# A hybrid encoder block in split float32: the two products with the high part of a weight tile put ahead of the one with the low part, and the memory rows loaded feature-wise

## The reference

```
h = rms_norm(x);  c_q, c_kv, k_rope, u_in, gate_a, gate_b = split(h @ w_in)
y_a = latent attention(c_q, c_kv, k_rope), 16 heads, chunk-causal
y_b = pointwise(silu(layer_norm(causal depthwise conv(glu(u_in)))))
x += (sigmoid(gate_a) * y_a + sigmoid(gate_b) * y_b) @ w_o
mem_n = rms_norm(mem)                      # 256 memory rows
k, v = split(mem_n @ w_kv_mem);  q = rms_norm(x) @ w_q_mem     # 4 heads of 512
x += softmax(q k^T * 512**-0.5) v @ w_o_mem
x += (silu(rms_norm(x) @ w_gate) * (rms_norm(x) @ w_up)) @ w_down   # d_ff 5632
return rms_norm(x)
```

## Time and profile before

| | us |
|---|---|
| median of 3 runs | 1680.53 (1680.05 to 1681.03) |
| the profiled execution | 1680.31 |
| its span, first to last instruction | 1678.5 |
| TensorE busy | 1662.8 (99% of the span) |
| VectorE, ScalarE, GpSimd busy | 1091.0, 818.9, 108.2 |
| TensorE weight loads | 1383.5 |
| TensorE's granted clock | 0.999 of full speed |

### The profile page before, as it was taken

How to read it: one execution, slowest core, us unless ns; L and a number is a source line. 1 busy time by engine, 2 the same in 40 slices (tenths; PEclk the granted TensorE clock), 3 DMA queues, 4 the chain that set the end, 5 groups by cost and what they waited for, 6 DMA issues and landing times.

```text
span 1678.5 us, 23555 instructions
## 1 busy us (share of the span) xinstructions
PE 1662.8 (99%) x7692; PEld 1383.5 (82%) x7692; DVE 1091.0 (65%) x1396; ACT 818.9 (49%) x1053; POOL 108.2 (6%) x160
## 2 busy tenths in 40 slices
PE   9999999999999999999999999999999999999998
PEld 8888888888888888878888788888888888888886
DVE  5555777678887457884448856666666666654453
ACT  7455655555545444555435644444444444344343
POOL 5100100011000000120001200000000000000000
PEclk9999999999999999999999999999999999999999
DMA  7865555555566655554445666666666666565563
GB/s 233 272 193 168 169 164 153 167 158 161 174 210 181 197 187 183 179 194 148 135 137 177 191 196 194 191 190 187 190 199 199 192 196 189 191 221 187 178 214 133
DMA packets 161284, 309.70 MB, mean 185 GB/s; under 512 B 10308, under 2 KB 17074, under 8 KB 160977
## 3 DMA queue, kind: packets, MB, share of 16 engines
q1 hardware_dynamic: 158864, 301.50, 57.8%
q0 software_dynamic: 1776, 6.47, 1.0%
q10 hardware_dynamic: 592, 1.06, 0.2%
HBM read 306.89 MB, written 2.10 MB: 184 GB/s over the span
## 4 chain that ended last, share of the span: by engine, by line
PE 92%; DVE 4%; issue 2%; ACT 1%; DMA 0%; DVEq 0%; SPq 0%; ACTq 0%; POOLq 0%; POOL 0%
PE acc L346 27%; PE acc L348 27%; PE acc L347 27%; DVE w_lo L1236 2%; PE tp L358 2%; DVE x_f L1549 1%; PE sc L675 1%; PE acc L569 1%; PE sc L491 1%; PE acc L571 1%; PE acc L570 1%; ACT w_hi L779 1%; PE acc L549 0%; PE acc L551 0%; PE acc L550 0%
## 5 line engine op out<-in xcount | busy, mean ns | idle before, releaser
L1236 DVE TENSOR_TENSOR w_lo<-raw,w_hi 128x1024 fp32r<-128x1024 f32 (+3 forms) x591 | 718.4, 1221 | 477.2 <-ACT w_hi L779 468.1
L779 ACT ACTIVATE w_hi<-raw 128x1024 fp32r<-128x1024 f32 (+3 forms) x591 | 606.5, 1029 | 767.3 <-PE acc L348 732.1
L346 PE MATMUL acc<-w_hi,crossT 128*128 128x512 f32 x832 | 325.7, 391 | 0.8 <-DVEq L1567 0.8
L348 PE MATMUL acc<-w_hi,crossT 128*128 128x512 f32 x832 | 323.9, 389 | 0.0
L347 PE MATMUL acc<-w_lo,crossT 128*128 128x512 f32 x832 | 323.8, 389 | 0.0
L346 PE MATMUL acc<-w_hi,mixT 128*128 128x512 f32 x796 | 315.5, 396 | 1.2 <-DVEq L1567 0.7
L348 PE MATMUL acc<-w_hi,mixT 128*128 128x512 f32 x796 | 310.5, 390 | 0.0
L347 PE MATMUL acc<-w_lo,mixT 128*128 128x512 f32 x796 | 310.1, 390 | 0.0
L346 PEld LDWEIGHTS acc<-w_hi,crossT 128*128 128x128 f32 x832 | 156.2, 188 | 33.7 <-issue 1.6
L348 PEld LDWEIGHTS acc<-w_hi,crossT 128*128 128x128 f32 x832 | 156.2, 188 | 32.7
L347 PEld LDWEIGHTS acc<-w_lo,crossT 128*128 128x128 f32 x832 | 156.2, 188 | 32.0
(11 more groups left out here) (244 smaller groups left out, 1350.9 us busy)
## 6 DMA issues: line engine op xcount, KB each, us to landing
raw<-in_w_in_dram SPq DMA_DIRECT2D x104, 512.0 KB, 3.7
raw<-in_w_gate_dram SPq DMA_DIRECT2D x88, 512.0 KB, 4.3
raw<-in_w_up_dram SPq DMA_DIRECT2D x88, 512.0 KB, 3.8
raw<-in_w_down_dram SPq DMA_DIRECT2D x80, 512.0 KB, 3.8
raw<-in_w_kv_mem_dram SPq DMA_DIRECT2D x64, 512.0 KB, 3.9
raw<-in_w_o_dram SPq DMA_DIRECT2D x32, 512.0 KB, 4.0
raw<-in_w_q_mem_dram SPq DMA_DIRECT2D x32, 512.0 KB, 3.7
raw<-in_w_o_mem_dram SPq DMA_DIRECT2D x32, 512.0 KB, 3.9
```

The source lines that it names most:

```text
L346: mm(o, lo, whi, start=first and k == 0, stop=False)
L348: ins = mm(o, hi, whi, start=False, stop=end)
L779: fn(w_hi[:, s, 0:width], raw[:, s, 0:width], ACT.Copy).then_inc(hi_done, 1)
L1236: V.tensor_tensor(w_lo[:, s, 0:width], raw[:, s, 0:width], w_hi[:, s, 0:width].bitcast(F32), ALU.subtract).then_inc(lo_done, 1)
```

## The change

- `products`: in each tile but a chunk's last it waits for `hi_done` alone, does the eight products with `w_hi` (for each bank and block low activations, then high ones), then waits for `lo_done` and does the four products with `w_lo`. The wait for `acc_free[1]` of a chunk's first tile stands in front of bank 1 as before. The last tile of a chunk is as it was. `tile_products` and `kv_products` (queries, keys and values of a pair) are as they were.
- The memory rows come from HBM already feature-wise (`memT`), as do the gains (`vecs`) and the taps (`w_dwT`); they are laid out outside the program. The 32 transposes of the memory rows and those of the gains and taps are gone. `operand_hi` and `operand_lo` make the parts on ScalarE and VectorE from `xs`. The squares of the memory rows are added up on VectorE (`fold_squares`, four additions) and summed over partitions by two products with a column of ones in the first pair.
- The memory attention: queries, keys, values and probabilities are split too, so each float32 product of 256 columns becomes three of the reduced type. This adds copies on ScalarE (`head_hi`, and the high part of the probabilities) and subtractions on VectorE (`head_lo` and others).
- Tables (`PAIR_*`, `HEAD_*`) say behind which tile a step of `attention` and of `mem_attention` stands in the loops. In H's first chunk the steps 0 to 4 stand behind tiles 0 to 4 as before.
- The bias row of the pointwise product is loaded at the start of D instead of in B.

```
+PAIR_PE = {1: (0, 1), 3: (2,), 6: (5,), 7: (7,)}
+PAIR_ACT = {1: (0, 1), 4: (3,), 6: (5,)}
+PAIR_DVE = {3: (2,), 4: (3,), 7: (7,)}
+HEAD_PE = {0: (0,), 2: (1,), 5: (3,), 6: (4,)}
+HEAD_ACT = {0: (0,), 2: (1,), 5: (3,), 6: (4,)}
+HEAD_DVE = {0: (0,), 2: (1,), 3: (2,), 5: (3,), 6: (4,)}
...
+                if not last:
+                    pe.wait_ge(hi_done, base + (t + 1))
+                    for b in range(NB):
+                        if first and not (isinstance(chunk, int) and chunk == 0):
+                            pe.wait_ge(acc_free[b], chunk)
+                        for k in range(kt):
+                            whi = w_hi[:, s, k * n:(k + 1) * n]
+                            for j in (1, 0):
+                                mm(acc[:, b, 0:n], lhs[j][:, k0 + k, b * P:(b + 1) * P], whi,
+                                   start=first and k == 0 and j == 1, stop=False)
+                    pe.wait_ge(lo_done, base + (t + 1))
+                    for b in range(NB):
+                        for k in range(kt):
+                            ins = mm(acc[:, b, 0:n], lhs[0][:, k0 + k, b * P:(b + 1) * P], w_lo[:, s, k * n:(k + 1) * n],
+                                     start=False, stop=False)
+                    ins.then_inc(tile_done, 1)
+                    return
                 pe.wait_ge(lo_done, base + (t + 1))
                 for b in range(NB):
-                    if first and not (isinstance(chunk, int) and chunk == 0):
-                        pe.wait_ge(acc_free[b], chunk)
                     for k in range(kt):
                         hi = lhs[0][:, k0 + k, b * P:(b + 1) * P]
                         lo = lhs[1][:, k0 + k, b * P:(b + 1) * P]
...
+                    if first and t == 5:
+                        pe.wait_ge(consts_made, 2)
+                        pe.wait_ge(sq_added, 1)
+                        for b in range(NB):
+                            ins = mm(xt[:, b:b + 1], sqT[:, 0, b * P:(b + 1) * P], ones[:, :], start=True, stop=True)
+                        ins.then_inc(sq_out, 1)
...
+                    for step in PAIR_PE.get(t, ()) if not first else ():
+                        attention(step, i - 1, i + (Q_C - 1))
...
-                    if last and t == 0:
-
-                        turn_x(0, Q_M0)
-                        turn_x(1, Q_M0)
                 kv_products(i * 12 + T_C, i * 3 + (C_C + 2))
-                if last:
-                    turn_x(2, Q_M0 + 1)
-                    turn_x(3, Q_M0 + 1)
 
             def kv_products(base, chunk):
...
+                    pe.wait_ge(key_lo, h + 1)
                     for b in range(NB):
                         for k in range(4):
-                            ins = mm(sc[:, 0, b * TOK:(b + 1) * TOK], memqT[:, k, b * P:(b + 1) * P],
-                                     memKT[:, cols(h * 4 + k, 1), :].rearrange("p o t -> p (o t)"),
-                                     start=k == 0, stop=k == 3)
+                            o = sc[:, 0, b * TOK:(b + 1) * TOK]
+                            hi, lo = (memqT[j][:, k, b * P:(b + 1) * P] for j in range(2))
+                            mm(o, lo, key_h[0][:, k, :], start=k == 0, stop=False)
+                            mm(o, hi, key_h[1][:, k, :], start=False, stop=False)
+                            ins = mm(o, hi, key_h[0][:, k, :], start=False, stop=k == 3)
...
+            def operand_hi(g):
+
+                dst, k0 = mem_rows(g)
+                for k in range(2):
+                    ins = fn(dst[0][:, k0 + k, :], mem_k[:, 2 * g + k, :], ACT.Copy, scale=vcol("norm_mem", 2 * g + k))
+                ins.then_inc(mem_hi, 1)
...
+                    if last and t == 9:
+                        act.wait_ge(tile_done, i * 12 + (T_C + 8))
+                    if last and t in (9, 11):
+                        operand_hi(t // 2 - 2)
+                    for step in PAIR_ACT.get(t, ()) if not first else ():
+                        attention(step, i - 1, i + (Q_C - 1))
...
+            def head_hi(t, h):
+
+                if t == 5:
+                    if not (isinstance(h, int) and h == 0):
+                        act.wait_ge(m_scores, h)
+                    fn(key_h[0][:, :, :], memKT[:, cols(h * 4, 4), :], ACT.Copy).then_inc(key_hi, 1)
+                if t == 6:
+                    if not (isinstance(h, int) and h == 0):
+                        act.wait_ge(m_pv, 2 * h)
+                    fn(val_h[0][:, :, :], memV[:, :, cols(h * CH, CH)], ACT.Copy).then_inc(val_hi, 1)
```

More of the change, by code:

```diff
@@ L235, in program @@
             ("m_norm", "m_turned", "m_out", "m_pv", "o_hi", "o_done"))
+        key_hi, key_lo, val_hi, val_lo, m_out_hi = (sem(n) for n in
+            ("key_hi", "key_lo", "val_hi", "val_lo", "m_out_hi"))
         x_new, x_turned, x_gained, x_hi_out, x_lo_out = (sem(n) for n in
@@ L705, in _ @@
                     turn_stage(Q_F, 2 * (S_F + 4))
-            for c in range(1, 4):
+            with pe.Fori(1, 4) as c:
                 for t in range(8):
                     products(c * 8 + T_G, t, 8, crossT, 2 * t, 2, CH, c + C_G)
-                    mem_attention(t, c - 1, c + (Q_G - 1))
+                    for step in HEAD_PE.get(t, ()):
+                        mem_attention(step, c - 1, c + (Q_G - 1))
             for t in range(8):
@@ L1147, in _ @@
                 split_hi(T_G, t + 4)
+                head_hi(t, 0)
                 if t == 1:
@@ L1154, in _ @@
                     split_hi(c * 8 + T_G, t + 4)
-                    mem_attention(t, c - 1, c + (Q_G - 1))
+                    for step in HEAD_ACT.get(t, ()):
+                        mem_attention(step, c - 1, c + (Q_G - 1))
+                    head_hi(t, c)
             for t in range(8):
@@ L1405, in gate_and_pair @@
                     split_lo(i * 12 + T_C, t + 4, width)
+                    if first and t in (0, 1, 2):
+                        fold_squares(t)
+                    if first and t == 2:
+                        fold_squares(3)
+                    if first and t < 2:
+                        operand_lo(t)
+                    if last and t in (9, 11):
+                        operand_lo(t // 2 - 2)
+                    if first and t == 6:
+                        dve.wait_ge(sq_out, 1)
+                        V.tensor_scalar(mean_sq[:, R_MEM, :], xt[:, 0:NB], 1.0 / D, EPS, ALU.mult, ALU.add)\
+                            .then_inc(ms_ready, 1)
                     if first and t == 3:
@@ L1410, in gate_and_pair @@
                         dve.wait_ge(zeros_made, 1)
-                    if not first:
-                        attention(t, i - 1, i + (Q_C - 1))
-                    if last and t == 8:
-                        x_lo(0, "norm_mem", H_M0 + 1)
-                        x_lo(1, "norm_mem", H_M0 + 2)
-                    if last and t == 11:
-                        x_lo(2, "norm_mem", H_M0 + 3)
-                        x_lo(3, "norm_mem", H_M0 + 4)
+                    for step in PAIR_DVE.get(t, ()) if not first else ():
+                        attention(step, i - 1, i + (Q_C - 1))
                     at = share_first if first else share_last if last else share
@@ L1520, in pointwise @@
                     split_lo(c * 4 + T_D, t + 4)
+                    if t == 2 and first:
+                        dve.wait_ge(row_in, 16)
                     if t == 2:
@@ L1585, in mem_attention @@
             def mem_attention(t, h, q):
+                if t == 0:
+                    for g in range(2):
+                        if g == 0 and not (isinstance(h, int) and h == 0):
+                            dve.wait_ge(m_scores, h)
+                        turned_lo_part(g, 2 * h + (H_G + g + 1), [[memqT[j][:, 2 * g:2 * g + 2, :]] for j in range(2)])
                 if t == 1:
@@ L1601, in mem_attention @@
                 if t == 3:
-                    dve.wait_ge(m_turned, h + 1)
-                    if not (isinstance(h, int) and h == 0):
-                        dve.wait_ge(m_pv, 2 * h)
-                    V.tensor_copy(probs_mT[:, :, :].rearrange("p k t -> p (k t)"), sc[:, 1, :]).then_inc(m_out, 1)
+                    dve.wait_ge(m_out_hi, h + 1)
+                    hi, lo = (probs_mT[j][:, :, :].rearrange("p k t -> p (k t)") for j in range(2))
+                    V.tensor_tensor(lo, sc[:, 1, :], hi.bitcast(F32), ALU.subtract).then_inc(m_out, 1)
                 if t == 4:
@@ L1620, in _ @@
                     split_lo(c * 8 + T_G, t + 4)
-                    mem_attention(t, c - 1, c + (Q_G - 1))
+                    for step in HEAD_DVE.get(t, ()):
+                        mem_attention(step, c - 1, c + (Q_G - 1))
+                    head_lo(t, c)
             dve.wait_ge(x_new, 4)
```

229 lines of the change are left out of this document (110 added, 119 removed).

## The result

The changed kernel takes 1686.37 us (median of 7 runs, 1686.22 to 1686.98), the kernel before 1680.53 beside it: a ratio of 1.0036, 95% interval 1.0025 to 1.0046. It is 5.8 us slower. The forecast was 1683.2 in a range of 1675.0 to 1688.0. The time lies in the range, but 3 us above the number, outside the forecast's own case (1680 to 1685, 0.50) and on the side that I had given 0.36. The profiled execution takes 1686.27, its span 1684.1 against 1678.5.

What follows compares the result with a forecast made beforehand. TensorE's own rate and what interrupts it were taken to bound the kernel. Savings of 10.4, boundary losses of 11.3 and additions of 1.8 gave +2.7 us on 1680.3, so 1683.0, stated as 1683.2; range 1675.0 to 1688.0.

Steps and rivals of the forecast that it cites:

- Bank 1 comes sooner: Chunk boundaries: bank 1 wanted by the fifth product, not the seventh, before its drain ends; 11.3 us lost, bounds 0 to 15.
- the general sum: Loss per boundary: drain's start after first product + duration + 0.06 (or 0.01) + 0.15 - 4 x 0.2266; 0.33 behind up chunks.
- The other parts: Everything besides the boundaries: 10.4 us taken off TensorE, 1.8 us added.
- Scores and values: Memory attention: 24 short products at 0.121 replace eight float32 ones in each of eight groups; 4.4 us saved.
- Transposes, the wait for `q_tok` and the new wait at E's start: Memory-row transposes gone, 3.5 us saved; last pair's `q_tok` wait shortened, 0.5 saved; operand copies delaying E, 0.8 added.
- The head loop: Wait before transposing probabilities gone in three G heads, 1.7 us saved; low parts add 0.3 in G, 0.2 in H.
- Squares: Two column sums of squares on TensorE, four short records: 0.3 us added.
- The start: Program start: second tile needn't wait for the low part, 0.3 us saved; gains load in smaller pieces, 0.2 added.
- products at their spacing: TensorE's line of work: each edit is worth the products, at their spacing, and waits it adds or removes; 0.2266 us a product.
- Rival 1: Chunk boundaries: bank 1's wait is covered, so the 11.3 us loss shrinks; 1671.7 with none, 1677 with half; chance 0.22.
- Rival 2: Scores and values: weight loads of 0.19 bound the 256-column products; 8.9 us more, 4.4 saving gone, 1696.5; chance 0.04.
- Rival 3: E's first chunk or head loop: ScalarE or VectorE falls behind; 3 to 5 us more, 1686 to 1688; chance 0.24.

Runs made afterwards that it cites:

- doubled: Changed kernel, but a chunk's first tile wants bank 1 by its third product in place of the fifth: 1713.37 us, ratio 1.0195 to the kernel before.
- the kernel with the old first tile: Changed kernel, but a chunk's first tile has the old product order, so bank 1 comes at the seventh product: 1674.44 us, ratio 0.9964.

## Why the prediction was right where it was, and where it was off

**The main step held.** "Bank 1 comes sooner" was the loss, and the runs show it from four sides: undone (12.1 less), alone (12.9 by the spans), undone in the first tile only (the same), and doubled (27.2 more). Sum: 11.3 predicted, 12.6 measured between the profiled executions.

**Its size was short at each boundary.** The starts of the products in the timeline show where. Behind the gate chunk at 1015.90 the fifth product comes 0.308 after the fourth and the sixth 0.338 after that, 0.08 and 0.11 over the usual 0.227; I had 0.08 and 0.10 (the times of rows 3 give 0.18; the general sum, with 0.15 for 0.14, made it 0.19). Behind the up chunk at 1037.87 they come after 0.458 and 0.335, 0.23 and 0.11 over; I had 0.22 and 0.10. What the sum lacked is the tail: the next products follow at up to 0.236, and it takes four of them in the first case and nine in the second until the step stays at 0.227. That is 0.02 more in the first case and 0.04 in the second, so 0.21 for my 0.19 and 0.38 for my 0.33. The chunks of the values and those into D to F lost 0.1 to 0.3, about as put; the boundary in a middle pair, which I had counted at 0.1, lost 0.10 to 0.20. Set product by product against the kernel with the old first tile, the first two of F and of H lost 0.30, 0.40, 0.33 and 0.43, where I had 0.27 at most. The two behind them, which should cost nothing because TensorE waits for bank 0 there, shortened that wait and gave back 0.30 in F and 0.26 in H, as put. The first of the keys, the first in D and the first of G lost nothing: at the last two TensorE waits longer for bank 0, and I had counted all four of G.

**The other parts were put at -8.6 and brought -7.0.** Point by point, by the moments at which bank 1 comes free:
- Scores and values: about 0.6 a group in place of 0.55. The scores come at 0.118, the values at 0.120, in place of 0.121. The line through 384 and 512 columns was the right guide.
- Transposes, the wait for `q_tok` and the new wait at E's start: 3.1 together, 3.2 predicted. The wait was 0.58 plus an exposed load, the 0.8 of the sum.
- The head loop: the wait for `probs_m` is gone in G and stays in H, as put. Against it, the values' first weight load waits 0.2 in each G head for the low part of the probabilities, but TensorE loses only 0.07 by it: the 24 products take 2.94 in G (787.55 to 790.49) and 2.87 in H, where nothing waits (870.75 to 873.62). That is 0.2 in all, where I had 0.3. H's scores lose 0.4 where I had 0.2.
- Squares: 0.5 in place of 0.3. Four short records take the chain from 158.97 to 159.31, and the next product pays for its restart.
- The start: nothing in place of 0.1, the 0.3 and 0.2 of the sum together. No run takes this part by itself.
- Not in the sum at all: 1.25 for `row_r`, 24 products and so 0.16 in each of the eight chunks of E. The sum took "products at their spacing" for granted, and the spacing is not the same for a buffer that lies otherwise. That is the one step that failed by kind and not by size.
- The time outside the span is 2.2 where it was 1.8: 0.35 more.

1.3 at the boundaries, 1.6 in the rest and 0.35 outside the span make 3.25, the 3.3 by which the profiled execution lies above its forecast of 1683.0. All three point the same way.

**The rivals.** Rival 1 (covered) fell: all but a few of the boundaries that I had counted show the wait, and the product behind one that waited comes 0.335 later. The load of the waiting product starts 0.04 after the increment (1038.97 to 1039.01), not before. Rows 5, on which the prediction rested this, don't show the load itself; this line of the kernel before does, 0.01 ahead of its product:

```profile
613.32 0.19 PEld L346 LDWEIGHTS acc<-w_hi,convT 128*128 128x128 f32 x1 [0.77 <-DVE stage L1496]
```

The Trainium skill ("TensorE: Matmul & The Clock Gate", Step-by-step) says that weight loads are pulled ahead of products in flight. The trace agrees between products without a wait, where load and product overlap throughout; behind a wait it doesn't show in the trace.

Rival 2 (a load bounds the short products) fell with the spacings of 0.118 and 0.120; its text gives 0.147 for 320 columns, where rows 7 give 0.145. Rival 3 gave 1686 to 1688, and the time landed there, but not for its reason: in E's first chunk TensorE waits 0.2 for VectorE, in the head loop for no copy of keys or values. A time alone would have confirmed the wrong story.

**What the profile was to show.** Mean spacing up by 5.8 over the stage's 22 boundaries: 5.8 over 20 of them, about 6.3 over all. The waits view was to show line 1173's and line 1645's successors, none over 0.3: it shows them for the weight loads, up to 0.3 and 0.5, not for the products. The fifth product was to come 0.3 to 0.5 after the fourth, then 0.33: 0.308 and 0.458, then 0.338 and 0.335.

## What to carry to other kernels

Where two accumulators are drained by turns, count the products between the first one of a chunk and the first that needs the second bank. Set the time that they take against the drain's start, its duration and the increment. If they fall short, add a restart (0.1 us in this kernel). An order that is neutral in work may shorten this cover at every boundary; reorder within a bank, not across the banks, or let the draining instruction increment the semaphore. When TensorE is busy 99% of the time, read the waits of its weight loads and the distance between two recurring instructions, not its own waits; take the loss itself from the starts of the products.

## What the runs showed of the hardware that I had not expected

- A product of 512 columns of the split type comes every 0.227 us where the stationary and the moving buffer lie a multiple of 512 bytes apart, and every 0.233 where they lie 192 bytes off such a multiple; here that cost 1.25 us. With 256 columns it is the other way round, 0.120 and 0.118. Why, no run shows.
- Behind a product that waited, TensorE loses 0.11 at the next product and 0.02 to 0.04 more over the four to nine behind it, which come at up to 0.236.
- Three products of the reduced type on 256 columns (0.354) are cheaper than one float32 product (0.431), also with all their weight loads.
